# First attention's weights: turned by TensorE, or by VectorE and transfers

## The chip, the cores and the metric

One core of a Trainium2 chip runs the kernel once. The metric is the device time of that execution in microseconds. The kernel before took 1275.75 us as the median of three runs (1275.66 to 1276.08). Its engines are TensorE (matmuls and their weight loads, output in PSUM), VectorE, ScalarE and GpSimd, each with a queue of instructions of its own that it works through in order; SyncE (SP) and ScalarE also issue transfers to the DMA engines from their queues. Engines wait for each other at semaphores that are counted up.

## The reference

Two blocks of a model on 512 tokens of width 1024, all float32. What matters here is the first block's attention, 8 heads of 64:

```python
for i in range(t // Q_BLOCK):                     # 4 query blocks of 128
    ctx = (i + 1) * Q_BLOCK
    z = einsum("bhqd,bhkd->bhqk", q_blk, k[:, :, :ctx]) * scale
    mask = k_pos[None, :] < q_pos[:, None]
    log_1m_beta = where(mask, log_sigmoid(-z), 0.0)
    cs = cumsum(log_1m_beta, axis=3)
    log_a = log_sigmoid(z) + (cs[..., -1:] - cs)
    a = where(mask, exp(log_a), 0.0)
    outs.append(einsum("bhqk,bhkd->bhqd", a, v[:, :, :ctx]))
```

Beside it the same block computes, from the same normed input, a gated projection (branch A: gelu, layer norm, a mixing over 128 tokens), a causal convolution of 31 taps over 512 channels (branch B), three gates per channel, and later a feed-forward part. The second block is not touched.

## The kernel before

Every large product is a split one: a float32 operand is divided into a high part (ScalarE's copy with rounding, `hi`, L708) and a low part (VectorE's difference, `lo`, L1160), and three matmuls are added (`split_mm`, L1905). Weights come in transfers of 1 MB on SP's queue, two units to a transfer, into two halves of STAGE; a transfer waits until the low part before it in the same half is made (L530). High and low parts stand in rings of four units: `hi(n + 4)` waits for unit n to be done, and TensorE's unit n + 4 waits for both parts.

The order of the work is written out by hand on each engine, one step for each unit. In the stretch around the change the units are the twelve of P, G and U (U_B, i = 0 to 11, banks 0 and 1 in turn) and then branch A (`branch(0)`: two halves q of six units r, four gate units and two quads that use BH and BL). The steps of first attention are threaded into them. There are 12 steps s, three for each pair p of heads (s = 3p, 3p + 1, 3p + 2), of 384, 384 and 512 columns for each head of the pair (`STEP_W`, L124). One step goes through these hands:

- TensorE, behind unit s + 1: `pair_scores(s)` (L2042) into banks 2 and 3, once the sigmoids of step s - 1 have been read from them.
- VectorE: `pair_mask(s)` (L1372); ScalarE: `pair_sigmoids(s)` (L805), 1 - beta into GB and beta into BT, two buffers each; VectorE: `pair_scan(s)` (L1384), the running product from the right, into RS; GpSimd: BT times RS (L654), the attention weights with queries on the partitions.
- TensorE, behind unit s + 3: `pair_turn(s)` (L2059) turns them in 6 or 8 tiles of 128x128 into banks 4 and 5; ScalarE: `pair_turned(s)` (L815) copies them into AT, keys on the partitions.
- TensorE, behind units 6, 9, 12 and 15: `pair_values(p)` (L2071) multiplies with VATT; ScalarE: `pair_out(p)` (L832) copies into ATT, which is branch(1)'s operand.

The units are numbered on through: 12 to 17 are the first half of branch A, 18 is r = 0 of its second half. Between these VectorE drains each unit out of PSUM (times RBC), and works through the 124 taps of the convolution (`taps`, L1340): so many in each step, given by the literals at L1429 and L1472. ScalarE does the gate activations with a table load where the function changes (L852). `gates_first` (L2131) follows behind branch(1), with the layer norm over the convolution.

Of the kernel before, what the change touches and what calls it, by code (L numbers as in the profile page):

```python
# [27 lines left out]
ALU = mybir.AluOpType  # L28
# [124 lines left out]
def program(nc, x, ln1_g, w_in, b_gate, sg_ln_g, sg_ln_b, sg_w, sg_b, w_a_out, cv_w, cv_b, cv_ln_g,  # L153
# [11 lines left out]
    with ExitStack() as ctx:  # L165
# [41 lines left out]
        RS = at("RS", [P, 2, SEQ], F32, 108)  # L207
        AT = at("AT", [P, 2, 1920], F32, 207)
# [64 lines left out]
        def sem(name):  # L273
# [36 lines left out]
                                                  sem("sc_scan"))  # L310
        a_ready, at_t, at_ready, av_done, att_read = (sem("a_ready"), sem("at_t"), sem("at_ready"),
# [3 lines left out]
        c_sum, c_mean, c_cent, c_sq, c_ssum, c_var, c_ve, c_sd, c_norm, c_ready = (  # L315
            sem("c_sum"), sem("c_mean"), sem("c_cent"), sem("c_sq"), sem("c_ssum"), sem("c_var"),
            sem("c_ve"), sem("c_sd"), sem("c_norm"), sem("c_ready"))
# [113 lines left out]
        def _(sp):  # L431
# [83 lines left out]
            for p, src in enumerate(transfers()):  # L515
# [29 lines left out]
                if p == U_B // 2 + 2:  # L545
                    qk_load(1)
                if p == 2:
# [65 lines left out]
        def _(pool):  # L613
# [30 lines left out]
            pool.wait_ge(rb_done, 1)  # L644
            pool.memset(SS[:], 0.0).then_inc(ss_clear, 1)

# [3 lines left out]
            for s in range(12):  # L650
# [3 lines left out]
                pool.tensor_tensor(b, b, RS[:, :, 0:STEP_W[s % 3]], ALU.mult).then_inc(a_ready, 1)  # L654
            squares(1)
# [38 lines left out]
        def _(act):  # L694
# [120 lines left out]
            def pair_turned(s):  # L815
                ty = s % 3
                act.wait_ge(at_t, s + 1)
                if ty == 0 and s:
                    act.wait_ge(av_done, s // 3)
                if ty == 0:  # L820
                    act.activation(AT[:, :, 0:256], PS[:, 4:6, 0:256], ACT.Copy).then_inc(at_ready, 1)
                    act.activation(AT[:, :, 512:640], PS[:, 4:6, 256:384], ACT.Copy).then_inc(at_ready, 1)
                else:
                    nk, c0 = ty + 2, 128 * (ty + 1)
                    act.activation(AT[:].rearrange("p a (k c) -> p a k c", c=384)[:, :, 0:nk, c0:c0 + P]
                                   if ty == 1 else
                                   AT[:, :, 384:384 + 384 * nk].rearrange("p a (k c) -> p a k c", c=384)
                                   [:, :, :, 0:P],
                                   PS[:, 4:6, 0:nk * P].rearrange("p a (k c) -> p a k c", c=P),
                                   ACT.Copy).then_inc(at_ready, 1)  # L830
# [24 lines left out]
            for b in range(2):  # L855
# [6 lines left out]
                for q in range(2):  # L862
                    for r in range(6):
                        n = U_C + 12 * b + 6 * q + r
                        hi(n + 4)
                        if b == 0 and q == 0 and r < 4:
                            stick_act(12 + r)
                        if q == 0 and r == (1, 0)[b]:
                            if b:
                                act.wait_ge(unit_done, n)  # L870
                            else:
                                act.wait_ge(sc_scan, 12)
                            act.activation(BH[:], src[:], ACT.Copy).then_inc(bh_ready, 1)
# [6 lines left out]
            for p in range(10):  # L880
# [20 lines left out]
                if p == 4:  # L901
                    act.wait_ge(c_ve, 1)
# [247 lines left out]
        def _(dve):  # L1150
# [232 lines left out]

            def pair_scan(s):  # L1384
# [16 lines left out]
            for i in range(12):  # L1401
# [15 lines left out]
                if 2 <= i < 13:  # L1417
                    pair_mask(i - 1)
                lo(U_B + i + 4)
# [8 lines left out]
                if i >= 4:  # L1428
                    taps(3 if i < 6 else 4)  # L1429
# [10 lines left out]
            for b in range(2):  # L1440
                for q in range(2):
                    for r in range(6):
# [29 lines left out]
                        taps((4, 4, 4, 4, 6, 3)[r])  # L1472

            assert taps_done == KW * CVK
            for p in range(10):
                if p < 9:
                    dve.wait_ge(unit_done, U_C + 24 + p + 1)
                if p < 8:
                    if p < 4:
                        dve.wait_ge(drained, DR_C + 28 + p + 1)  # L1480
                    else:
                        dve.wait_ge(av_done, 4)
                        dve.wait_ge(at_ready, 16)
# [14 lines left out]
                if p == 3:  # L1498
# [5 lines left out]
                    dve.tensor_tensor(TG0[:], TG0[:], UU[:, 3, :], ALU.add).then_inc(c_ssum, 1)  # L1504
                if p == 4:
                    dve.wait_ge(c_var, 1)
                    dve.tensor_scalar(TG0[:], PS[:, 5, :], 1.0 / W, EPS, ALU.mult, ALU.add)\
                       .then_inc(c_ve, 1)
# [392 lines left out]
        def _(pe):  # L1901
# [157 lines left out]
            def pair_turn(s):  # L2059

                pe.wait_ge(a_ready, s + 1)
                if s:
                    pe.wait_ge(at_ready, s + (s + 2) // 3)
                else:
                    pe.wait_ge(sg_read, 4)
                for par in range(2):
                    for z in range(STEP_W[s % 3] // P):
                        last = tr(PS[:, 4 + par, z * P:(z + 1) * P], BT[s % 2][:, par, z * P:(z + 1) * P])
                last.then_inc(at_t, 1)

            def pair_values(p):  # L2071

                pe.wait_ge(at_ready, 4 * p + 4)
# [324 lines left out]
```

## Time and profile before

| | before |
|---|---|
| median of three runs | 1275.75 us |
| profiled execution, its own time | 1275.76 us |
| its span, first to last instruction | 1274.0 us |
| TensorE matmul busy | 1263.9 us, 99% |
| VectorE busy | 869.3 us, 68% |
| ScalarE busy | 586.3 us, 46% |
| GpSimd busy | 88.1 us, 7% |
| mean of the DMA engines (the queue of SP and ScalarE) | 40.7% |

Busy time is an average over stages with different limits. The span in 40 slices of 31.85 us shows them, in tenths of each slice (9 is 90% or more):

```
PE   8999999999999999999999999999999999999998
DVE  5489899899877776666666333675469998655544
ACT  7235466232263443333333223512368899444223
DMA  7556222422322333323322222249825555665421
```

PE is TensorE, DVE VectorE, ACT ScalarE. The stage of the change is in slices 4 to 8.

### The profile page before, as it was taken

To read this page: it belongs to the slowest core of one execution; us is meant where nothing else is said; L and a number is where in the kernel's file an instruction comes from. 1 tells how busy PE (TensorE), PEld (TensorE's weight loads), DVE (VectorE), ACT (ScalarE), POOL (GpSimd) and SP (SyncE) were. 2 spreads that over 40 slices of the span, in tenths; PEclk is the share of its full clock that TensorE was granted. 3 is DMA by queue.
4 is the path that set the end of the run, shared out by engine and by line. 5 is a ranking of instruction groups with operands and counts; after the bars stand their busy time and mean duration, and the time that the engine had idled before them with its cause. 6 is when DMAs were issued, how large, how long until landed. Compare 5 with 4: busy or idle time off the path is not lost.

```text
span 1274.0 us, 15378 instructions
## 1 busy us (share of the span) xinstructions
PE 1263.9 (99%) x5760; PEld 1016.6 (80%) x5760; DVE 869.3 (68%) x1164; ACT 586.3 (46%) x866; POOL 88.1 (7%) x68
## 2 busy tenths in 40 slices
PE   8999999999999999999999999999999999999998
PEld 7888777888888888888888888888877777777886
DVE  5489899899877776666666333675469998655544
ACT  7235466232263443333333223512368899444223
POOL 0000222000000200000000001300012220000000
PEclk9999999999999999999999999999999999999999
DMA  7556222422322333323322222249825555665421
GB/s 264 178 130 172 66 67 67 165 97 77 120 75 97 99 100 99 99 99 99 98 91 102 90 88 91 99 125 215 239 76 124 140 159 131 183 148 149 161 70 67
DMA packets 220922, 153.36 MB, mean 120 GB/s; under 512 B 119704, under 2 KB 196416, under 8 KB 220608
## 3 DMA queue, kind: packets, MB, share of 16 engines
q1 hardware_dynamic: 220272, 151.53, 40.7%
q10 hardware_dynamic: 592, 1.05, 0.2%
q8 instruction: 37, 0.61, 0.2%
q14 instruction: 21, 0.17, 0.0%
HBM read 134.21 MB, written 18.35 MB: 120 GB/s over the span
## 4 chain that ended last, share of the span: by engine, by line
PE 97%; DVE 1%; DMA 1%; ACT 0%; SPq 0%; issue 0%; ACTq 0%
PE PS L1903 97%; PE PS L1970 1%; DMA STAGE<-in_w_in 1%; DVE WL L1163 0%; DVE XL L1201 0%; DVE XG L1193 0%; ACT XH L744 0%; ACT WH L716 0%; DVE TB L1752 0%; DVE XT L1896 0%; ACT SQF L1133 0%; DVE XT L1891 0%; DVE BLR L1790 0%; SPq L521 0%; SPq L520 0%
## 5 line engine op out<-in xcount | busy, mean ns | idle before, releaser
L716 ACT ACTIVATE WH<-STAGE 128x1024 fp32r<-128x1024 f32 x214 | 225.9, 1058 | 540.2 <-PE PS L1903 528.6
L1903 PE MATMUL PS<-XH,WH 128*128 128x512 f32 x960 | 380.9, 397 | 0.0
L1163 DVE TENSOR_TENSOR WL<-STAGE,WH 128x1024 fp32r<-128x1024 f32 x214 | 275.4, 1289 | 147.8 <-ACT WH L716 147.4
L1903 PE MATMUL PS<-XH,WL 128*128 128x512 f32 x960 | 373.9, 389 | 0.0
L1903 PE MATMUL PS<-XL,WH 128*128 128x512 f32 x960 | 373.8, 389 | 0.0
L1903 PEld LDWEIGHTS PS<-XH,WH 128*128 128x128 f32 x960 | 180.2, 188 | 43.5 <-issue 5.5
L1903 PEld LDWEIGHTS PS<-XL,WH 128*128 128x128 f32 x960 | 180.3, 188 | 39.0 <-issue 2.6
L1903 PEld LDWEIGHTS PS<-XH,WL 128*128 128x128 f32 x960 | 180.2, 188 | 38.1
L1903 PE MATMUL PS<-WH,XH 128*128 128x512 f32 x224 | 88.1, 393 | 0.6 <-DVE WL L1163 0.6
L1903 PE MATMUL PS<-WH,XL 128*128 128x512 f32 x224 | 87.2, 389 | 0.0
L1903 PE MATMUL PS<-WL,XH 128*128 128x512 f32 x224 | 87.2, 389 | 0.0
L1354 DVE SCALAR_TENSOR_TENSOR CACC<-CPAD,VEC,CACC 128x512 f32<-128x512 f32 x120 | 84.3, 765 | 0.0
L1579 DVE TENSOR_TENSOR UPB<-PS,RBC 128x512 f32<-128x512 f32 x44 | 30.4, 690 | 70.7 <-PE PS L1903 70.6
L1903 PE MATMUL PS<-FH,WH 128*128 128x512 f32 x176 | 68.5, 389 | 0.0
L1903 PE MATMUL PS<-FL,WH 128*128 128x512 f32 x176 | 68.5, 389 | 0.0
L1903 PE MATMUL PS<-FH,WL 128*128 128x512 f32 x176 | 68.5, 389 | 0.0
L639 POOL TENSOR_TENSOR SS<-SS,SQ 128x512 f32<-128x512 f32 x16 | 22.7, 1420 | 572.2 <-ACT SQ L725 572.2
L1903 PEld LDWEIGHTS PS<-WH,XH 128*128 128x128 f32 x224 | 42.1, 188 | 9.8 <-ACT XCM L738 1.0
L1903 PEld LDWEIGHTS PS<-WL,XH 128*128 128x128 f32 x224 | 42.1, 188 | 8.8 <-issue 0.2
L1903 PEld LDWEIGHTS PS<-WH,XL 128*128 128x128 f32 x224 | 42.0, 188 | 8.8
L932 ACT ACTIVATE YB<-UPB,VEC 128x512 f32<-128x512 f32 x44 | 35.3, 803 | 12.1 <-DVE UPB L1579 12.1
L1903 PEld LDWEIGHTS PS<-FH,WL 128*128 128x128 f32 x176 | 33.0, 188 | 6.9
(289 smaller groups left out, 1782.3 us busy)
## 6 DMA issues: line engine op xcount, KB each, us to landing
STAGE<-in_w_in SPq DMA_DIRECT2D x51, 1024.0 KB, 5.2
STAGE<-in_w_up SPq DMA_DIRECT2D x22, 1024.0 KB, 5.1
STAGE<-in_w_down SPq DMA_DIRECT2D x11, 1024.0 KB, 5.0
probabilities<-TB SPq DMA_DIRECT2D x48, 128.0 KB, 5.8
PT<-probabilities SPq DMA_DIRECT2D x18, 256.0 KB, 5.6
STAGE<-in_w_out SPq DMA_DIRECT2D x4, 1024.0 KB, 5.3
STAGE<-in_w_rnn_out SPq DMA_DIRECT2D x4, 1024.0 KB, 5.3
STAGE<-in_w_attn_out SPq DMA_DIRECT2D x4, 1024.0 KB, 5.3
```

What stands on the lines that cost most here:

```text
L639: pool.tensor_tensor(SS[:], SS[:], SQ[:], ALU.add).then_inc(ss_added, 1)
L716: act.activation(ring(WH, n), staged(n), ACT.Copy).then_inc(hi_done, 1)
L932: act.activation(YB[:, r, :], UPB[:, r, 4:516], ACT.Identity, scale=VEC[:, bass.ds(V_FW[2] + c, 1)], bias=VEC[:, bass.ds(V_FB + c, 1)]).th ...
L1163: dve.tensor_tensor(ring(WL, n), staged(n), ring(WH, n).bitcast(F32), ALU.subtract)\
L1354: ins = dve.scalar_tensor_tensor(CACC[:, c, :], CPAD[:, c, 2 + j:2 + j + SEQ], col(V_CVW + KW * j + c), CACC[:, c, :], ALU.mult, ALU.add)
L1579: dve.tensor_tensor(UPB[:, r, 4:516], PS[:, r, :], RBC[:], ALU.mult)\
L1903: return pe.matmul(out_, lhsT, rhs, start=start, stop=stop, skip_group_check=True)
L1970: return pe.transpose(out_, in_, IDENT[:])
```

## The change

In a few words: "First attention's weights turned by VectorE and transfers, loaded through ScalarE's queue, three tiles in turn; tokens stay unscaled, fourteen taps moved". TensorE's turn and ScalarE's copies go. VectorE transposes BT in blocks of 32x32 into BTT (three tiles in turn and a fourth for step 11) in its step s + 3; SP stores each tile with 128-byte pieces to memory, four DMAs a step, behind the transfers p = 13 to 19; ScalarE waits for the three stores of a pair and loads them into AT with eight DMAs, in units 7, 10, 13 and 16. The values move to units 9, 12, 15 and 18, with bank 3 in place of 6 for pair 2. Two taps a unit stand where three or four did, five where four did. The clearing of SS is moved behind the last product on GpSimd, since BTT0 lies over it, and some semaphores of the convolution's norm are merged.

```diff
+        BTT = [at("BTT0", [P, 1024], F32, 91), at("BTT1", [P, 1024], F32, 175), at("BTT2", [P, 1024], F32, 184),
+               at("BTT3", [P, 1024], F32, 100)]
+        AROW = [nc.dram_tensor(f"attention_rows{i}", [1024, P], F32, kind="Internal").ap()
+                for i in range(12)]
+        def pair_tile(s):
+            return BTT[3 if s == 11 else s % 3][:, 0:2 * STEP_W[s % 3]]
...
+            def at_store(s):
+                sp.wait_ge(at_t, s + 1)
+                for a in range(4):
+                    sp.dma_start(AROW[s][0:2 * STEP_W[s % 3]].rearrange("(b i) (a j) -> a i b j", i=32, j=32)[a],
+                                 pair_tile(s)[32 * a:32 * a + 32].rearrange("p (b j) -> p b j", j=32))\
+                      .then_inc(at_out[s % 3], 16)
...
+                step = p - U_B // 2 - 5
+                if 0 <= step < 7:
+                    for s in ((0,), (1, 2), (3, 4), (5, 6), (7, 8), (9, 10), (11,))[step]:
+                        at_store(s)
...
+            def at_load(p):
+                for i in range(3):
+                    act.wait_ge(at_out[i], 64 * (p + 1))
+                if p:
+                    act.wait_ge(av_done, p)
+                for s in range(3 * p, 3 * p + 3):
+                    w = STEP_W[s % 3]
+                    for par in range(2):
+                        rows_ = AROW[s][par * w:(par + 1) * w].rearrange("(k p) c -> p k c", p=P)
+                        if s % 3 == 0:
+                            act.dma_start(AT[:, par, 0:256].rearrange("p (k c) -> p k c", c=P), rows_[:, 0:2])\
+                              .then_inc(at_ready, 16)
+                            act.dma_start(AT[:, par, 512:640], rows_[:, 2]).then_inc(at_ready, 16)
...
             def pair_out(p):
                 act.wait_ge(av_done, p + 1)
-                act.activation(ATT[:, p, :], PS[:, (6, 7, 6, 2)[p], :], ACT.Copy).then_inc(att_read, 1)
+                if p == 2:
+                    act.wait_ge(at_out[1], 64 * 4)
+                act.activation(ATT[:, p, :], PS[:, (6, 7, 3, 2)[p], :], ACT.Copy).then_inc(att_read, 1)
             def stick_act(i):
                 if 1 <= i < 13:
                     pair_sigmoids(i - 1)
-                if i >= 6 and i % 3 == 0:
-                    pair_out(i // 3 - 2)
-                if 3 <= i < 15:
-                    pair_turned(i - 3)
+                if i >= 9 and i % 3 == 0:
+                    pair_out((i - 9) // 3)
+                if i >= 7 and i % 3 == 1:
+                    at_load((i - 7) // 3)
...
+            def pair_turn(s):
+                w = STEP_W[s % 3]
+                dve.wait_ge(a_ready, s + 1)
+                if s >= 3:
+                    dve.wait_ge(at_out[s % 3], 64 * (s // 3))
+                dve.transpose(pair_tile(s).rearrange("p (a c) -> p a c", c=w), BT[s % 2][:, :, 0:w])\
+                   .then_inc(at_t, 1)
...
                 if 2 <= i < 13:
                     pair_mask(i - 1)
+                if i >= 3:
+                    pair_turn(i - 3)
                 lo(U_B + i + 4)
...
-                    taps(3 if i < 6 else 4)
+                    taps(2)
...
+                        if b == 0 and q == 0 and r < 3:
+                            pair_turn(9 + r)
                         lo(n + 4)
...
+                            if b == 0 and q == 0:
+                                for k in range(3):
+                                    dve.wait_ge(at_out[k], 64 * 4)
...
-                        taps((4, 4, 4, 4, 6, 3)[r])
+                        taps((5, 5, 5, 5, 5, 3)[r])
...
             def pair_values(p):
-                pe.wait_ge(at_ready, 4 * p + 4)
-                if p == 2:
-                    pe.wait_ge(att_read, 1)
-                if p == 3:
+                pe.wait_ge(at_ready, 128 * p + 128)
+                if p >= 2:
                     pe.wait_ge(sig_ready, 24)
...
-                if i >= 6 and i % 3 == 0:
-                    pair_values(i // 3 - 2)
-                if 3 <= i < 15:
-                    pair_turn(i - 3)
+                if i >= 9 and i % 3 == 0:
+                    pair_values((i - 9) // 3)
```

## Rows read from the trace of the kernel before

**Rows 1.** The page's part 4, by line: the chain that ended last.
```profile
PE PS L1903 97%; PE PS L1970 1%; DMA STAGE<-in_w_in 1%; DVE WL L1163 0%; DVE XL L1201 0%; DVE XG L1193 0%; ACT XH L744 0%; ACT WH L716 0%; DVE TB L1752 0%; DVE XT L1896 0%; ACT SQF L1133 0%; DVE XT L1891 0%; DVE BLR L1790 0%; SPq L521 0%; SPq L520 0%
```

**Rows 2.** Timeline of TensorE: start us, us, engine, line, operation, count.
```profile
111.43 0.93 PE L1903 MATMUL PS<-QKT 64*128 64x128 f32 x8
112.28 0.50 PE L1903 MATMUL PS<-XH,WH 128*128 128x512 f32 x1
...
136.29 0.93 PE L1903 MATMUL PS<-QKT 64*128 64x128 f32 x8
...
137.77 0.47 PE L1903 MATMUL PS<-XH,WH 128*128 128x512 f32 x1
...
143.43 0.92 PE L1903 MATMUL PS<-QKT 64*128 64x384 f32 x4
...
145.13 0.48 PE L1903 MATMUL PS<-XH,WH 128*128 128x512 f32 x1
...
200.13 2.37 PE L1903 MATMUL PS<-AT,VATT 128*64 128x512 f32 x16
...
208.64 0.82 PE L1970 MATMUL PS<-IDENT,BT 128*128 128x128 f32 x6
...
214.78 1.04 PE L1970 MATMUL PS<-IDENT,BT 128*128 128x128 f32 x8
...
221.23 2.37 PE L1903 MATMUL PS<-AT,VATT 128*64 128x512 f32 x16
```

**Rows 3.** Busy time in one stretch: PE, PEld, DVE, ACT, POOL, clock, DMA share, GB/s.
```profile
129.04:223.37 94.33, 94.33 (x484) 69.28 (x484) 86.24 (x111) 59.58 (x71) 22.51 (x11) 1.00 0.21 68
```

**Rows 4.** Timeline of VectorE.
```profile
71.75 2.48 DVE L1262 STREAM_TRANSPOSE QK<-QK 128x512 f32<-128x512 f32 x4
...
162.02 1.22 DVE L1163 TENSOR_TENSOR WL<-STAGE,WH 128x1024 fp32r<-128x1024 f32 x1
...
168.20 0.67 DVE L1410 TENSOR_TENSOR TG<-PS,RBC 128x512 f32<-128x512 f32 x1
...
169.12 2.23 DVE L1163 TENSOR_TENSOR WL<-STAGE,WH 128x1024 fp32r<-128x1024 f32 x1
...
171.88 2.73 DVE L1354 SCALAR_TENSOR_TENSOR CACC<-CPAD,VEC,CACC 128x512 f32<-128x512 f32 x4
...
176.24 0.66 DVE L1410 TENSOR_TENSOR TG<-PS,RBC 128x512 f32<-128x512 f32 x1
...
208.02 3.54 DVE L1354 SCALAR_TENSOR_TENSOR CACC<-CPAD,VEC,CACC 128x512 f32<-128x512 f32 x2
```

**Rows 5.** Timeline of GpSimd.
```profile
168.44 1.83 POOL L654 TENSOR_TENSOR BT<-BT,RS 128x768 f32<-128x768 f32 x1 [7.38 <-DVE RS L1395]
```

**Rows 6.** Timeline of ScalarE.
```profile
186.67 1.28 ACT L811 ACT_TABLE_LOAD   x1
187.97 0.81 ACT L811 ACTIVATE GB<-PS 128x768 f32<-128x768 f32 x1
...
191.50 0.63 ACT L852 ACTIVATE TG<-TG 128x512 f32<-128x512 f32 x1
```

**Rows 7.** Timeline of SP's queue: the time is that of the issues.
```profile
225.22 0.37 SPq L531 DMA_DIRECT2D STAGE<-in_w_a_out x1
...
986.44 0.39 SPq L531 DMA_DIRECT2D STAGE<-in_w_in  x1
...
987.97 5.93 SPq L477 DMA_DIRECT2D probabilities<-TB  x4
```

**Rows 8.** Busy time in one stretch, as rows 3.
```profile
994.00:996.00 2.00, 2.00 (x8) 1.08 (x6) 1.97 (x5) 1.99 (x7) 0.00 (x0) 1.00 0.75 123
```

**Rows 9.** ScalarE's own DMAs: issue ns (min/median/max), then KB and us to landing.
```profile
L1145 ACTq DMA_DIRECT2D out<-XT x4: 350/368/383, 1257.7 to 1270.8; - x4
...
out<-XT ACTq DMA_DIRECT2D x4, 256.0 KB, 2.6
```

**Rows 10.** Span and mean granted TensorE clock.
```profile
core 0: 1274.0 us, clock 0.999
```

More of the change, by code:

```diff
@@ L314, in program @@
         tg_act, tg_used = sem("tg_act"), sem("tg_used")
-        c_sum, c_mean, c_cent, c_sq, c_ssum, c_var, c_ve, c_sd, c_norm, c_ready = (
-            sem("c_sum"), sem("c_mean"), sem("c_cent"), sem("c_sq"), sem("c_ssum"), sem("c_var"),
-            sem("c_ve"), sem("c_sd"), sem("c_norm"), sem("c_ready"))
+        c_sum, c_mean, c_cent, c_sq, c_sd, c_norm, c_ready = (
+            sem("c_sum"), sem("c_mean"), sem("c_cent"), sem("c_sq"),
+            sem("c_sd"), sem("c_norm"), sem("c_ready"))
         bh_ready, bl_ready = sem("bh_ready"), sem("bl_ready")
@@ L654, in _ @@
                 pool.tensor_tensor(b, b, RS[:, :, 0:STEP_W[s % 3]], ALU.mult).then_inc(a_ready, 1)
+            pool.wait_ge(at_out[0], 64 * 4)
+            pool.memset(SS[:], 0.0).then_inc(ss_clear, 1)
             squares(1)
@@ L813, in pair_sigmoids @@
                 act.activation(BT[s % 2][:, :, 0:w], PS[:, 2:4, 0:w], ACT.Sigmoid).then_inc(sig_ready, 1)
[L815 to L830, printed above, removed]
+            def at_load(p):
[11 more added lines that the diff above has]
+                            act.dma_start(AT[:, par, 512:640], rows_[:, 2]).then_inc(at_ready, 16)
+                        elif s % 3 == 1:
+                            act.dma_start(AT[:, par, 0:1152].rearrange("p (k c) -> p k c", c=384)[:, :, 256:384],
+                                         rows_).then_inc(at_ready, 16)
+                        else:
+                            act.dma_start(AT[:, par, 384:1920].rearrange("p (k c) -> p k c", c=384)[:, :, 0:P],
+                                         rows_).then_inc(at_ready, 16)
@@ L865, in _ @@
                         hi(n + 4)
-                        if b == 0 and q == 0 and r < 4:
-                            stick_act(12 + r)
+                        if b == 0 and (q == 0 or r == 0):
+                            stick_act(12 + 6 * q + r)
                         if q == 0 and r == (1, 0)[b]:
@@ L872, in _ @@
                                 act.wait_ge(sc_scan, 12)
+                                act.wait_ge(at_out[2], 64 * 3)
                             act.activation(BH[:], src[:], ACT.Copy).then_inc(bh_ready, 1)
@@ L901, in _ @@
                 if p == 4:
-                    act.wait_ge(c_ve, 1)
+                    act.wait_ge(c_sum, 3)
                     act.activation(TG0[:], TG0[:], ACT.Sqrt).then_inc(c_sd, 1)
@@ L2057, in pair_scores @@
                 last.then_inc(sc_done, 1)
[L2059 to L2069, printed above, removed]
             def pair_values(p):
-                pe.wait_ge(at_ready, 4 * p + 4)
-                if p == 2:
-                    pe.wait_ge(att_read, 1)
-                if p == 3:
+                pe.wait_ge(at_ready, 128 * p + 128)
+                if p >= 2:
                     pe.wait_ge(sig_ready, 24)
@@ L2080, in pair_values @@
                         h = 2 * p + par
-                        last = mm(PS[par * DH:(par + 1) * DH, (6, 7, 6, 2)[p], kb * P:SEQ],
+                        last = mm(PS[par * DH:(par + 1) * DH, (6, 7, 3, 2)[p], kb * P:SEQ],
                                   VATT[:, kb, h * DH:(h + 1) * DH], AT[:, par, 512 * kb:384 * kb + SEQ],
@@ L2118, in branch @@
                             pe.wait_ge(drained, DR_C + 16 * b + 8 * q - 8 + r + 1)
+                            if b == 0 and r == 2:
+                                pe.wait_ge(att_read, 4)
                         cm_unit(n0 + 6 * q + r, r % 2 if b == 0 and q == 0 else r, XH, XL)
-                        if b == 0 and q == 0:
-                            stick_pe(12 + r)
+                        if b == 0 and (q == 0 or r == 0):
+                            stick_pe(12 + 6 * q + r)
                     if b == 0 and q == 0:
-                        pe.wait_ge(att_read, 3)
+                        pe.wait_ge(att_read, 2)
                     if q == 0:
@@ L2140, in gates_first @@
                     if p == 4:
-                        pe.wait_ge(c_ssum, 1)
-                        mm(PS[:, 5, :], ONES[:], TG0[:], True, True).then_inc(c_var, 1)
+                        pe.wait_ge(c_sum, 2)
+                        mm(PS[:, 5, :], ONES[:], TG0[:], True, True).then_inc(c_mean, 1)
                 pe.wait_ge(c_cent, KW)
-                pe.wait_ge(c_ve, 1)
+                pe.wait_ge(c_sum, 3)
                 pe.wait_ge(bh_ready, 3)
```

10 lines of the change are left out of this document (4 added, 6 removed).

## The prediction

> **What bounds the kernel now.** I read the chain that ended last first. It is TensorE for 97% of the span in its split matmuls and another 1% in its transposes [rows 1]. So a microsecond of TensorE work that goes is a microsecond of time, unless another engine or a transfer becomes late. The second view is TensorE's own order of work around first attention [rows 2]. The stage runs in channel-major units of 24 matmuls (5.45 us). Behind unit i stand the scores of step i-1, every third time the values of a head pair, and the transposes of step i-3. I count the units on: 0 to 11 are the P, G and U columns, 12 to 17 the first half of branch 0, 18 the first of its second half. The third view is VectorE, which does one step of work per unit. From its drain of unit 3 (129.04) to its drain of unit 15 (223.37) it is busy 86.2 us of 94.3 [rows 3], and at the end of the stretch it is behind: unit 15 is done at 221.23 [rows 2] and drained 2.1 us later. TensorE never waits for it, but little is free there. ScalarE and the queues come last in the reading.
>
> **Off TensorE.** With 6 tiles the turn lies between scores and unit: 136.29 to 137.77 against 111.43 to 112.28 where none stands, 1.48 less 0.85, so 0.63. With 8 tiles it is 143.43 to 145.13 less 0.85, so 0.85. Alone between units, 208.64 to 214.78 less a unit is 0.69, and 214.78 to 221.23 less a unit is 1.00 [rows 2]. Seven of the first, three of the second and the last two make 8.65 us. All twelve lie on the path. The values move three units later (2.3 us each, the same sixteen matmuls), which costs nothing by itself. Of the path 8.65 us go, if nothing is late.
>
> **On VectorE.** 12 transposes come in. Four of 128x512 take 2.48 us one behind another, 0.62 each [rows 4]; by width that is 0.93 and 1.24 us for 768 and 1024 columns, of which some 0.07 lies over the neighbour: 8 x 0.87 and 4 x 1.16, 11.6 us (bounds 8 and 16). A tap is 0.66 (2.73 for four) [rows 4]. Two a unit in place of three or four is 14 fewer up to unit 11, 9.2 us; five in place of four gives one back in each of the units 12 to 14.
>
> There is a third term. The weights' low part (two SBUF operands) takes 2.23 us when GpSimd's product runs beside it, against 1.22 alone; the drain just before it, with one operand in PSUM, keeps 0.67 beside the same product [rows 4, 5]. In the new order a transpose stands between mask and low part, so GpSimd is through (1.83 us) before the low part begins. The nearest row for a one-operand instruction is that drain, so I let the transpose keep its time: some 1 us less in each of units 8, 9, 11 and 0.5 in 10 and 12. If it is stretched instead, as the low part is, those 4 us come back on VectorE and reach TensorE at pair 3: 1277.9 in place of the sum below. The Trainium skill, "SBUF — State Buffer", section "Who interferes with whom", says that a VectorE instruction with two SBUF inputs contends with a GpSimd instruction that reads SBUF, and one with at most one SBUF input doesn't, outside the two-port modes. By that the transpose is free of it, which is the case that I take from the drain's row; the trace agrees for low part and drain and shows no transpose there.
>
> **Step by step.** A unit's period is 6.5 us with scores (143.43 less 136.29 less 0.63), 6.7 behind the 512-wide scores, 9.0 where values stand as well, and 5.45 alone. Unit 5 ends at 142.1 (143.43 less two turns), and then units 6 to 10 at 148.6, 155.3, 161.8, 168.3, 177.3 and 11 at 183.8. VectorE's step behind unit 8 took 8.04 us (168.20 to 176.24) [rows 4]; less 1.3 for two taps and 1.0 for the low part, with 1.16 for the transpose, it is 6.9, and its neighbours come out at 6.7 to 7.5 in the same way; it starts them at 142.5, 149.3, 156.1, 163.3, 170.2, 177.4, 184.5. It keeps up.
>
> **ScalarE's queue.** It now holds the loads behind the sigmoids in units 7, 10, 13 and 16: eight DMAs each time. An issue on this queue was 0.37 us for 256 KB [rows 9], on SP's 0.37 to 0.39 for weights and 1.5 for the stores of second attention behind a full ring [rows 7]; I take 0.45, so 3.6 us (bounds 3.0 and 7). Removed are the copies out of PSUM of the same units. In unit 7 nothing is late. In unit 10 the sigmoids end at 177.3 + 5.1, the loads at 186.0, and the table load and Gelu of that unit (1.28 and 0.55) [rows 6] at 187.9. Only then come the next high part (188.9), table load and two sigmoids of 0.75 [rows 6]: 191.7. TensorE wants them for its scores when unit 12 ends, at 190.3: **1.4 us of stall** (bounds 0 and 4). VectorE waits for that high part too and starts step 12 at about 194.4.
>
> Step 12 on VectorE has drain, mask, transpose, low part, the 512-wide scan and five taps of which two run beside GpSimd's product (3.54 us for two in the same place before, 1.4 alone) [rows 4], and a wait for the sigmoids: 11.7 us, so step 13 starts at 206.1. Unit 13 ends at 190.3 + 1.4 + 9.0 = 200.7. Step 13 takes 8.1 us (BL's low part in it, five taps, a transpose), step 14 6.2. Unit 15 needs the drain of unit 13 (206.7) and could start at 206.2: 0.4 us more (bounds 0 and 2). So step 15 starts at 220.4, with unit 15 done at 212.0. That step's low part, done at 222.2, releases the weights' transfer and behind it on SP's queue the store of the last step, as it released the transfer at 225.22 before [rows 7].
>
> **The last round trip.** The values of pair 3 stand behind unit 18, which ends at 212.0 + 2.35 (values 2) + 3 x 5.45 = 230.7. They need the last store, then the loads. Nearest is second attention's: weights issued 986.44, two loads of 256 KB, four stores with 4096 packets of 128 bytes, the DMA engines through at about 995.5 (busy 0.75 of 994 to 996) [rows 7, 8]. Less 1.4 for those loads that is 7.7 us from the low part. The eight loads: the last is issued 3.2 us later and lands 2.6 after that, as ScalarE's stores did [rows 9]; 5.8. Landed at 222.2 + 7.7 + 5.8 = 235.7: **5.0 us of stall** (bounds 0, if VectorE is 5 us earlier, and 10, if the loads meet a full ring as the four stores did, 5.93 us for four issues in place of 1.8 [rows 7]). ScalarE stands still meanwhile, from about 221 to 234, its high part for unit 21 among what is behind, but that is not wanted before 248. The earlier loads of pair 2 (their stores land near 200, their wait begins near 202) are in time, and BH with its low part comes 3 us before its quads. The stall lets VectorE catch up by as much, and from the quads on it has fewer instructions a unit than 5.45 us hold, so the taps that were moved there (2 us more in each half branch) stay hidden; without that cover they would cost those 2 us.
>
> Removed semaphores, other banks for pair 2 (3 in place of 6), SS cleared later and the merged c_* waits change no order on a busy path; zero, bounds -0.3 and +0.3. The diff holds no edit of how tokens are scaled, so nothing is counted for it.
>
> Sum: 8.65 gained, 1.4 + 0.4 + 5.0 lost, 1.85 left. The profiled execution took 1275.76 us around its span of 1274.0, the runs' median is 1275.75; so 1275.76 - 1.85 = **1273.9 us**.
>
> **The rivals.** First, VectorE and ScalarE have room after all: drains that start late but never stop TensorE, issues of 0.37, a shorter last trip. For it: TensorE waited nowhere before, and VectorE had 8.1 us of idle time in the stretch [rows 3]. Against: TensorE comes 8.65 us sooner, which takes up all of that idle time. With 2 us of stalls in all it gives 1269.1.
>
> Second, on the other side, the load on ScalarE's queue: it waits in order for stores that wait behind weights and behind VectorE, and holds back high parts and TensorE alike. The point from which it decides is a trip of 15.4 us from the low part of step 15 to the last landing, where I have 13.5: the stall at pair 3 is then 6.9 and the gain is gone. At 20 us, which a full ring (7 us of issues) and stores 3 us slower would give, it is 11.5 and the time 1280.4. For it: four such stores held SP's queue for 5.93 us [rows 7], and what waits for them now waits on the engine that feeds TensorE. Against: the loads have a queue of their own, with nothing ahead of them.
>
> Third, TensorE's clock. It was granted 0.999 of full over the span [rows 10], which is some 3 us at the lower of its two levels, and in the stage it was 1.00 with TensorE never idle. A stop of 5 us behind unit 18 has no like in this trace after the start. If the lower level (1.2 GHz) followed for half a unit or for a whole one, the matmuls, 0.227 us apart now, would be at least twice 0.21 apart: 2.4 to 4.8 us, time 1276.3 to 1278.7. The Trainium skill, "TensorE: Matmul & The Clock Gate", section "HAM oscillation — how this bites in real kernels", holds that an idle gap in mid-kernel can send the clock back to the lower level; no row of before can show it.
>
> **How the numbers follow.** The forecast has 0.45, around 1273.9, itself from 1271.5 to 1276.3; the first rival 0.20; ScalarE's queue 0.20; the clock 0.15. What a measurement can tell from no change is 0.2%, 2.55 us, so faster means under 1273.2. The forecast gives 0.19 to faster, 0.26 to the same; the first rival 0.20 to faster; the second 0.01 to the same and 0.19 to slower; the third 0.11 to the same and 0.04 to slower. Together 0.39, 0.38, 0.23. The range leaves out the tails of both ends: 1269.3 to 1279.
>
> **What would show it.** No TensorE transposes after 30 us, the chain in pieces of 6.5 us. A gap of TensorE of 5 us ahead of the values of pair 3, released by a DMA into AT, and one of 1.4 ahead of the scores behind unit 12, released by ScalarE. VectorE's transposes at 0.9 and 1.2 beside GpSimd, and low parts of 1.2 behind them. ScalarE's eight issues at 0.45. A granted clock under 1.00 behind the gap speaks for the third rival. The forecast is wrong if the gaps sum to under 4 or over 9 us, or if a gap stands at another place, the quads of branch 0 above all.

## The result, and the profile after

The changed kernel takes **1279.34 us** (median of 9 runs, 1278.46 to 1280.84), the kernel before beside it 1275.61 (9 runs, 1275.32 to 1276.08): ratio 1.0029, 95% interval [1.0020, 1.0038]. It is 3.7 us slower. The forecast was 1.85 us faster; the measured time lies just outside its range. The profiled execution took 1280.36 us around a span of 1278.6.

The first views of the kernel after, answering to [rows 10] and [rows 1] (span and clock; the chain by line):
```profile
core 0: 1278.6 us, clock 0.995
```
```profile
PE PS L1945 93%; DMA STAGE<-in_w_in 1%; DVE CACC L1381 0%; DVE WL L1190 0%; SPq L508 0%; DMA attention_rows<-BTT 0%; ACTq L850 0%; DMA AT<-attention_rows 0%; DVE XL L1228 0%; DVE XG L1220 0%; ACT WH L736 0%; ACTq L848 0%; ACTq L853 0%; ACT XH L764 0%; ACTq L846 0%
```
The transposes (1% of the chain before) are gone, but TensorE's share fell from 97% to 93%: the chain now leaves it for VectorE, SP's queue, two transfers and ScalarE's queue. Where it leaves it, the waits of TensorE say (us in total, times, longest), and its timeline, which answers to [rows 2]:
```profile
PE PS L1945 <- DMA AT<-attention_rows: 6.5, 1, 6.5
PE PS L1945 <- ACT BT L833: 2.2, 1, 2.2
```
```profile
192.92 1.67 PE L1945 MATMUL PS<-QKT 64*128 64x512 f32 x4 [2.25 <-ACT BT L833]
194.52 3.48 PE L1945 MATMUL PS<-AT,VATT 128*64 128x512 f32 x16
197.93 0.50 PE L1945 MATMUL PS<-XH,WH 128*128 128x512 f32 x1
...
214.48 2.37 PE L1945 MATMUL PS<-AT,VATT 128*64 128x512 f32 x16
...
239.86 4.54 PE L1945 MATMUL PS<-AT,VATT 128*64 128x512 f32 x16 [6.47 <-DMA AT<-attention_rows]
244.33 0.60 PE L1945 MATMUL PS<-XH,WH 128*128 128x512 f32 x1
```
Two stops stand there, at the two places that the prediction named. But look at the durations too: the same sixteen matmuls of a pair's values take 2.37, 3.48 and 4.54 us, and the scores 1.67 where they take 1.13 in the stage otherwise. The clock granted in those microseconds (the column behind the five engines) explains it:
```profile
192.00:193.00 1.00, 0.08 (x2) 0.08 (x2) 1.00 (x2) 0.98 (x3) 0.00 (x0) 1.00 0.61 70
193.00:194.00 1.00, 1.00 (x4) 0.22 (x4) 1.00 (x2) 1.00 (x1) 0.00 (x0) 0.69 0.86 276
194.00:196.00 2.00, 2.00 (x6) 0.52 (x6) 2.00 (x4) 1.23 (x3) 0.92 (x1) 0.50 1.08 364
196.00:197.00 1.00, 1.00 (x6) 0.37 (x4) 1.00 (x3) 0.62 (x1) 1.00 (x1) 0.61 1.37 215
197.00:198.00 1.00, 1.00 (x13) 0.49 (x7) 1.00 (x2) 0.55 (x1) 0.21 (x1) 1.00 1.50 187
...
237.00:238.00 1.00, 0.00 (x0) 0.00 (x0) 0.03 (x1) 1.00 (x2) 0.00 (x0) 0.87 0.87 254
238.00:244.00 6.00, 4.14 (x16) 1.72 (x16) 6.00 (x9) 0.82 (x1) 0.00 (x0) 0.50 0.86 278
244.00:245.00 1.00, 1.00 (x6) 0.59 (x3) 1.00 (x2) 0.55 (x2) 0.00 (x0) 0.71 1.18 492
```
0.50 is the lower level, 1.2 GHz. Behind the first stop the clock fell during the scores and came back before the values were through (0.61 at 196, 1.00 at 197); at the second it fell while TensorE still stood, and came back behind the values.

**The balance.** Set the starts of the split matmuls of both kernels side by side, the first with the first, and read where the difference changes. It falls by 0.6 or 0.84 at each turn that is gone, in all by 8.4 us. At the start of unit 12 it is -8.50: nine turns (6.2), and one pair's values (2.3), which now come later. At unit 13 it is -5.14: a stop of 2.25 and 1.6 at the lower clock, less a turn of 0.6. At unit 15 it is -6.75. At unit 19 it is +4.56: the values that moved here (2.3), the stop of 6.5, 2.2 at the lower clock, and 0.3 left over. From there to the end nothing changes any more. The turns gave 8.4; the stops took 8.7 and the clock 3.8, and some 0.5 at the stops is not put down to any row: +4.6, which is the difference of the two spans.

### The profile page after: what moved, and what is told of

Same layout as the page of the kernel before. It is cut to its first block, busy times and chain, and to the rows that moved or that the text cites. A ratio compares the mean times of both kernels' runs of the same rounds, so it can differ in the third digit from the quotient of the medians.

```text
span 1278.6 us, 15300 instructions
## 1 busy us (share of the span) xinstructions
PE 1260.3 (99%) x5680; PEld 1010.1 (79%) x5680; DVE 875.4 (68%) x1176; ACT 576.3 (45%) x850; POOL 88.5 (7%) x68
## 4 chain that ended last, share of the span: by engine, by line
PE 93%; DVE 2%; DMA 1%; ACTq 1%; ACT 1%; SPq 1%; issue 0%
PE PS L1945 93%; DMA STAGE<-in_w_in 1%; DVE CACC L1381 0%; DVE WL L1190 0%; SPq L508 0%; DMA attention_rows<-BTT 0%; ACTq L850 0%; DMA AT<-attention_rows 0%; DVE XL L1228 0%; DVE XG L1220 0%; ACT WH L736 0%; ACTq L848 0%; ACTq L853 0%; ACT XH L764 0%; ACTq L846 0%
## 5 line engine op out<-in xcount | busy, mean ns | idle before, releaser
L1190 DVE TENSOR_TENSOR WL<-STAGE,WH 128x1024 fp32r<-128x1024 f32 x214 | 271.0, 1269 | 148.7 <-ACT WH L736 148.4
L1945 PEld LDWEIGHTS PS<-FH,WH 128*128 128x128 f32 x176 | 33.0, 188 | 6.9
```

The source lines that it names most:

```text
L1190: dve.tensor_tensor(ring(WL, n), staged(n), ring(WH, n).bitcast(F32), ALU.subtract)\
L1945: return pe.matmul(out_, lhsT, rhs, start=start, stop=stop, skip_group_check=True)
```

## The experiments

Each time stands beside runs of the kernel before on the same chip, 1275.8 to 1276.0 in all of them; ratios are to these. The kernel after was measured twice, with 1279.34 and, further below, 1280.89 us, so a difference of about 1 us between kernels that keep a stop is not read as a gain or a loss. Traces begin up to 1.2 us apart ahead of the stage: where two are set side by side, both are counted from their first scores (111.42 in the kernel after).

### Matmuls that keep TensorE busy in both stops

```diff
+            def fill(n, bank):
+                for _ in range(n):
+                    mm(PS[:, bank, :], XH[:, 0, 0:P], XH[:, 0, :], True, True)
...
             def stick_pe(i):
+                if i == 12:
+                    fill(9, 4)
+                if i == 18:
+                    pe.wait_ge(att_read, 3)
+                    fill(26, 3)
```


> The changed kernel with needless matmuls (0.227 us each) in TensorE's two gaps: 9 ahead of the scores behind unit 12, 26 ahead of the values of pair 3. Nothing else is changed, and the two waits stay as they are. First theory (two stops, and the clock falls in each): the gaps stay as long in sum, filled now, the granted clock stays 1.00 in both places, and the 1.6 and 2.2 us that scores and values took longer at the lower level come back, so 1279.3 - 3.8 = 1275.5. Rival (the longer values and scores are slowed by something else, transfers or PSUM, and the clock's level only stands beside it): no change, 1279.3. If the filling reaches past a gap, up to 0.5 us is lost.

Measured 1279.83 us (6 runs), ratio 1.0033 [1.0020, 1.0045]: no gain. TensorE in that trace:
```profile
193.27 1.13 PE L1945 MATMUL PS<-QKT 64*128 64x512 f32 x4 [0.32 <-ACT BT L833]
194.33 2.37 PE L1945 MATMUL PS<-AT,VATT 128*64 128x512 f32 x16
...
208.58 0.50 PE L1945 MATMUL PS<-XH,WH 128*128 128x512 f32 x1 [0.78 <-DVE GS L1487]
...
233.01 6.05 PE L1945 MATMUL PS<-XH 128*128 128x512 f32 x26
...
240.91 2.38 PE L1945 MATMUL PS<-AT,VATT 128*64 128x512 f32 x16 [1.85 <-DMA AT<-attention_rows]
```
The clock stayed at 1.00 and scores and values have their full speed, so the stops do cause the lower clock. But the 3.8 us did not come back. Half of the first 1.6 went at unit 15, where TensorE now came early enough to wait 0.78 us for VectorE's drain of unit 13 (GS). The rest only makes TensorE wait longer at pair 3, where the end of the stop is set by a transfer: AT landed at 240.9 in place of 239.8, or 0.8 later from the first scores on. Of the second 2.2, this landing took 0.8 and 0.9 more went at 1085 us of the span, in the second attention, where TensorE waited 1.6 for VectorE's BLR in place of 0.6.

### The stores ahead of the wait for the low part

```diff
+                step = p - U_B // 2 - 5
+                if 0 <= step < 7:
+                    for s in ((0,), (1, 2), (3, 4), (5, 6), (7, 8), (9, 10), (11,))[step]:
+                        at_store(s)
                 if p >= 2:
                     sp.wait_ge(lo_done, 2 * p - 2)
                 sp.dma_start(STAGE[:, p % 2, :].rearrange("p (k c) -> p k c", k=kd, c=ncol), src)\
...
-                step = p - U_B // 2 - 5
-                if 0 <= step < 7:
-                    for s in ((0,), (1, 2), (3, 4), (5, 6), (7, 8), (9, 10), (11,))[step]:
-                        at_store(s)
```


> The changed kernel with each store of attention rows issued ahead of the weights' transfer of its place, so it waits for its own transpose only and not for VectorE's low part and 1 MB of weights. First theory (the stop at pair 3 is the round trip low part, weights, store, load): store 11 leaves at 218 in place of 224.7, the loads end at about 231, before unit 18 ends at 233.3, so the gap of 6.5 us and the 2.2 us of lower clock go; the gap behind unit 12 stays (2.3 + 1.6): 1279.3 - 8.9 = 1270.4. Rival (the volume of small packets on the DMA engines, 5.2 MB in 128 bytes, is what is late): the same bytes in another order, 1279.3 within 1 us. Second rival (VectorE's lag itself): the gap shrinks by under 3 us.

Measured 1270.21 us (4 runs), ratio 0.9954 [0.9938, 0.9971]: 5.7 us faster than before, 9.1 than the kernel after, where 1270.4 was expected. At pair 3 the difference to the kernel before now changes by 2.37 us, the values alone: no stop. With the same bytes in another order this also rules out the rival of DMA volume. The way there was not as expected. TensorE waits for AT behind unit 9 now, 1.1 us, and as it comes that much later and ScalarE's sigmoids 1.2 earlier, the stop behind unit 12 is gone as well; 0.7 appears at unit 15, on VectorE's drain. So the mechanism at pair 3 is confirmed, and that the number fits to 0.2 us is partly luck.

### The loads on SP's queue

ScalarE's eight issues (`at_load`) go to SP, behind the stores that they wait for; nothing else is changed.
```diff
-                if i >= 7 and i % 3 == 1:
-                    at_load((i - 7) // 3)
...
-                        at_store(s)
+                    for kind, k in ((("s", 0),), (("s", 1), ("s", 2), ("l", 0)), (("s", 3), ("s", 4)),
+                                    (("s", 5), ("l", 1), ("s", 6)), (("s", 7), ("s", 8), ("l", 2)),
+                                    (("s", 9), ("s", 10)), (("s", 11), ("l", 3)))[step]:
+                        (at_store if kind == "s" else at_load)(k)
```


> The changed kernel with the loads of attention rows issued by SP's queue in place of ScalarE's, the stores where they were. First theory (the stop behind unit 12 is ScalarE's 4 us of issues ahead of a high part and two sigmoids): that gap of 2.3 us goes with its 1.6 us of lower clock; VectorE comes some 3 us earlier too, so the gap at pair 3 stays 6.5 to 7.5 us, with its lower clock: 1279.3 - 3.3 = 1276.0. Rival (the sigmoids are late because VectorE's mask and transpose are late): the gap behind unit 12 stays over 1.5 us, and 1279.3 stays.

Measured 1278.79 us (10 runs), ratio 1.0021 [1.0011, 1.0031]; 1276.0 was expected. TensorE's waits and the values of pair 3:
```profile
PE PS L1945 <- DMA AT<-attention_rows: 6.9, 1, 6.9
PE PS L1945 <- ACT BT L856: 1.4, 3, 0.8
```
```profile
238.42 4.21 PE L1945 MATMUL PS<-AT,VATT 128*64 128x512 f32 x16 [6.86 <-DMA AT<-attention_rows]
```
The stop behind unit 12 shrinks to 0.8 and its clock stays up, so ScalarE's issues were the greater part of its cause. It is worth little by itself. TensorE waits 0.3 us for the sigmoids behind units 10 and 11 too, and 0.8 at unit 15 for VectorE's drain. Unit 18 ends 1.3 us earlier, counted from the first scores, but the trip takes 16.0 us here (low part done at 222.4, last load landed at 238.4), and so the stop at pair 3 grows from 6.5 to 6.9 and brings the lower clock again. The expectation had that stop and its clock, but neither the longer trip nor the small waits; the median is only 0.55 us below the kernel after, which the two measurements of that kernel do not tell from nothing.

### Both

```diff
+                    for kind, k in ((("s", 0),), (("s", 1), ("s", 2)), (("s", 3), ("s", 4)),
+                                    (("s", 5), ("l", 1), ("s", 6)), (("s", 7), ("s", 8)),
+                                    (("s", 9), ("s", 10)), (("s", 11), ("l", 3)))[step]:
+                        (at_store if kind == "s" else at_load)(k)
                 if p >= 2:
                     sp.wait_ge(lo_done, 2 * p - 2)
```
The loads of pairs 0 and 2 stand behind the transfers of steps 1 and 4.

> Both edits: stores ahead of the weights' transfers and loads on SP's queue. First theory: no stop of TensorE is left in the stage, the clock stays at 1.00, and what was taken off TensorE (8.4 us) is the whole difference: 1275.6 - 8.4 = 1267.2 (to 1268.5 if a wait of under 1 us shows up). Rival (DMA volume, or VectorE as the bound): a gap of 3 us or more remains and the time is over 1271.

Measured **1267.92 us** (4 runs), ratio 0.9936 [0.9920, 0.9953]: 8.0 us faster than before, and the fastest version of all. TensorE waits nowhere in the stage:
```profile
190.71 1.13 PE L1949 MATMUL PS<-QKT 64*128 64x512 f32 x4
191.76 2.37 PE L1949 MATMUL PS<-AT,VATT 128*64 128x512 f32 x16
...
229.90 2.38 PE L1949 MATMUL PS<-AT,VATT 128*64 128x512 f32 x16
```
With no stop left, the balance against the kernel before is the 8.4 us of the turns less some 0.6 in small steps. So the turns are worth their time and VectorE can carry its transposes; what ate the gain was the order of stores and loads on two queues.

### The last store alone

```diff
+                step = p - U_B // 2 - 5
+                if 0 <= step < 7:
+                    for s in ((0,), (1, 2), (3, 4), (5, 6), (7, 8), (9, 10), (11,))[step]:
+                        if s in (11,):
+                            at_store(s)
                 if p >= 2:
                     sp.wait_ge(lo_done, 2 * p - 2)
...
-                        at_store(s)
+                        if s not in (11,):
+                            at_store(s)
```


> The kernel after with one line of order changed: SyncE issues the last store of attention_rows (of step 11 alone) ahead of its wait for the low part of step 14 and the transfer of the weights, the ten stores before it stay where they were. Theory (pair 3's values wait for a round trip that runs low part, weights, store, load): the stop of 6.5 us ahead of them goes, and with it the 2.2 us that they took longer at the lower clock, while the stop of 2.3 us ahead of the scores behind unit 12 stays, being ScalarE's eight load issues. 1279.3 - 9.0 = about 1270.5 us. Rival (all the stores together were what held, by filling SyncE's queue): the stop at pair 3 shrinks by 1 or 2 us only, about 1278. Rival (the stop behind unit 12 hangs on the stores too): it goes as well, about 1268 to 1269.

Measured 1270.72 us (5 runs), ratio 0.9962 [0.9948, 0.9976]; 1270.5 was expected. One store's place is worth 8.6 us. Its trace holds a surprise:
```profile
192.96 1.13 PE L1951 MATMUL PS<-QKT 64*128 64x512 f32 x4 [2.14 <-ACT BT L839]
194.02 2.37 PE L1951 MATMUL PS<-AT,VATT 128*64 128x512 f32 x16
```
The stop behind unit 12 is there, 2.1 us, and the clock did not fall. So this kernel and the kernel after were each run again.

> The kernel with the last store alone ahead of the transfer of the weights, a second time, for its granted clock behind unit 12. If the clock there stands by the stop's place in time and not by its length, the scores and values may take 5 us in this execution where they took 3.4 in the first. Otherwise 3.4 us again. The time is near 1270.7 us, or 1.6 more with the lower clock.

> The kernel after, unchanged, a second time. Theory that the stop of 2.3 us behind unit 12 always brings the lower clock: the scores and values behind it take 5 us again and the granted clock is near 0.50 from 194 to 196 us. Rival, since the kernel with the last store first had a stop of 2.1 us there at a granted clock of 1.00: whether such a short stop brings it differs from execution to execution, and here it may be 3.4 us. In either case the stop of 6.5 us at pair 3 brings it again, and the median is 1279 to 1280 us.

The last store first, a second time, took 1271.66 us (one run):
```profile
192.28 1.13 PE L1951 MATMUL PS<-QKT 64*128 64x512 f32 x4 [2.28 <-ACT BT L839]
193.34 4.07 PE L1951 MATMUL PS<-AT,VATT 128*64 128x512 f32 x16
```
```profile
194.00:196.00 2.00, 2.00 (x8) 0.61 (x6) 2.00 (x5) 1.22 (x2) 1.56 (x1) 0.50 1.18 305
```
Here it fell, for the same instructions in the same order. The kernel after, a second time, had 1280.89 us (5 runs), ratio 1.0037 [1.0022, 1.0051], a stop of 2.15 with the clock at 0.50 behind it, and 8.2 at pair 3. So a stop of some 2.2 us brings the lower level in four of the five traces that have one there, and not in the fifth. Its length does not set the fifth apart: one of 2.06 us behind unit 9, in a run below, brought it too. What does is left open.

### Matmuls in one stop only

Nine ahead of the scores behind unit 12, on top of the last store first:
```diff
             def stick_pe(i):
+                if i == 12:
+                    fill(9, 4)
```


> The kernel of the run before (last store first), with nine more matmuls of 128x512 f32r ahead of the scores behind unit 12, into a bank that nobody reads then; they compute nothing that is used. Theory that the lower clock in the scores and values behind unit 12 is time lost: with no round trip behind it that eats the gain, the scores and values take 3.4 us instead of 5.0 and the time falls by about 1.3 to 1.6 us against the run before. Rival (the time from there on is set by VectorE's or the transfers' row, not by TensorE): within 0.5 us of the run before.

And the 26 ahead of pair 3's values, on top of the kernel after:
```diff
             def stick_pe(i):
+                if i == 18:
+                    pe.wait_ge(att_read, 3)
+                    fill(26, 3)
```


> The kernel after with 26 more matmuls of 128x512 f32r ahead of the values of pair 3 alone, into a bank that nobody reads then; the stop behind unit 12 is left as it was. They compute nothing that is used and end before the load of AT lands, so they move no transfer. Theory that the values of pair 3 pay for the lower clock in time: they take 2.4 us instead of 4.5, and the time falls by 2 us against the kernel after, to about 1277.3 us. Rival (what is won here is lost again at the round trip of the second attention's probabilities, near 1085 us of the span, where both kernels with filler so far came 0.9 to 1.2 us later): 1278 to 1279.5 us.

The first took 1271.34 us (5 runs), ratio 0.9966 [0.9952, 0.9981], no better than without them, though its profiled clock is 1.00 behind unit 12; its trace also has 0.9 us more at 1085 us. The two traces of the last store first show the price of that fall better, as their program is the same. The one in which it fell is 1.7 us later at unit 13 and only 0.7 later behind unit 15, mostly since there the other waits 0.78 for VectorE's drain; at pair 3 it waits 0.64 for AT and is 1.4 later from there on. The spans differ by 0.6 (1269.9 against 1269.3), as the traces begin 0.7 apart. One execution each is little to go by. The second took 1279.77 us (10 runs, one of them a lone 2579.5 that stays unexplained), ratio 1.0028 [1.0018, 1.0038]: no clear gain, 1.1 us below the kernel after on the same chip (1280.89), in spreads that overlap. The fill was too short there:
```profile
232.51 6.05 PE L1945 MATMUL PS<-XH 128*128 128x512 f32 x26
241.25 4.07 PE L1945 MATMUL PS<-AT,VATT 128*64 128x512 f32 x16 [2.69 <-DMA AT<-attention_rows]
```
The 2.69 us that were left of the stop brought the lower clock back, so the trace did not test what it was made for, while the 1.85 us left in the run with both fills did not bring it. Its other executions say more: the five with a mean clock of 0.999 took 1277.8 to 1279.6 us, the four with 0.997 or 0.998 took 1280.0 to 1282.0. A longer stop makes both the time longer and a fall likelier, so this is no price of the clock alone.

### The fourteen taps

In the kernel before, moved as in the change:
```diff
-                    taps(3 if i < 6 else 4)
+                    taps(2)
...
-                        taps((4, 4, 4, 4, 6, 3)[r])
+                        taps((5, 5, 5, 5, 5, 3)[r])
```


> The kernel before with only the fourteen taps moved: two each of units 4 to 12, five each of the first five steps of the second branch. Attention's weights are turned by TensorE as before. Theory: TensorE doesn't wait for VectorE there, the taps run beside other work in either place, so no change, 1275.5 to 1276 us. Rival (the moved taps themselves make step 12 to 15 of VectorE late, and this is what the changed kernel pays): 1 to 4 us slower.

And in the kernel after, put back:
```diff
+                if s == 11:
+                    dve.wait_ge(at_t, 11)
...
-                    taps(2)
+                    taps(3 if i < 6 else 4)
...
-                        taps((5, 5, 5, 5, 5, 3)[r])
+                        taps((4, 4, 4, 4, 6, 3)[r])
```


> The kernel after with the fourteen taps where they were before (three or four a unit in units 4 to 12, four a step behind them), so the turns, transfers and loads stay and the move of the taps is undone. Theory: VectorE's steps 4 to 12 grow by 1.1 to 2.2 us each, the turns come later, ScalarE's loads behind unit 12 too, and TensorE waits there and at unit 13 longer than now: slower than the kernel after by 3 to 12 us, 1282 to 1291 us. Rival (VectorE's steps have room, and the round trip at pair 3 sets the time alone; the steps behind unit 12 are shorter with four taps): pair 3 is earlier, 1277 to 1279 us.

The added wait, of VectorE for its own turns before the last, changes no order. The first took 1275.89 us (10 runs), ratio 1.0001 [0.9992, 1.0011]: by itself the move does nothing. The second took 1285.08 (4 runs), ratio 1.0071 [1.0054, 1.0088], 5.7 us over the kernel after. TensorE's waits:
```profile
PE PS L1947 <- ACT BT L833: 6.0, 3, 3.3
PE PS L1947 <- DMA AT<-attention_rows: 5.9, 1, 5.9
```
Three stops behind ScalarE's sigmoids in place of one. So with these queues the transposes would not fit on VectorE without the move of the taps; both numbers are as they were expected.

## Why the prediction was wrong

**Off TensorE: right.** 8.65 us were forecast, 8.4 went. Nothing of the twelve turns was hidden.

**VectorE and the third term: right.** Transposes cost what their width says, and keep it beside GpSimd's product; the low part behind them meets only the product's end. VectorE and GpSimd in unit 8, against [rows 4, 5]:
```profile
170.89 0.97 DVE L1417 STREAM_TRANSPOSE BTT<-BT 128x768 f32<-128x768 f32 x1
171.78 1.33 DVE L1190 TENSOR_TENSOR WL<-STAGE,WH 128x1024 fp32r<-128x1024 f32 x1
```
```profile
170.20 1.83 POOL L672 TENSOR_TENSOR BT<-BT,RS 128x768 f32<-128x768 f32 x1 [4.95 <-DVE RS L1431]
```
0.97 was put at 0.93, and it is 0.96 at 208.11, where no product runs. The low part is 1.33 where it was 2.23, and 1.18 where nothing runs beside it. The rule of the Trainium skill's "SBUF — State Buffer", section "Who interferes with whom", holds here for the transpose, an operation that the trace before could not show.

**ScalarE's queue: 2.25 us in place of 1.4.** ScalarE in the kernel after, from the first load to the sigmoids for the scores behind unit 12:
```profile
183.12 0.37 ACTq L846 DMA_DIRECT2D AT<-attention_rows  x1
...
186.07 1.07 ACTq L853 DMA_DIRECT2D AT<-attention_rows  x2
187.17 1.28 ACT L878 ACT_TABLE_LOAD   x1 [4.16 <-issue]
...
192.06 0.80 ACT L833 ACTIVATE BT<-PS 128x768 f32<-128x768 f32 x1
```
The issues took 4.0 us (forecast 3.6, at 0.45 each; 0.50 measured) and began 0.7 later than forecast. The step is right in kind, and the run with the loads on SP confirms it. The 0.4 at unit 15 did not occur here, where TensorE came later by the stop and the lower clock; it did, with 0.71 to 0.78 us, in the five traces in which the clock stayed up and TensorE had waited at unit 9, 10 or 12 (both fills, all stores first, loads on SP, the last store first, and the same with one fill). So that term's mechanism was right, and it is what took half of the first fall of the clock back.

**The last round trip: the step that failed.** Its last load was to land at 235.7 and landed at 239.8, and the stop before it was 6.5 us in place of 5.0. The chain of waits in the kernel after, where it leaves TensorE (start us, us, what):
```profile
223.12 1.14 DVE WL L1190
...
224.28 0.39 SPq L548
...
224.72 0.51 SPq L508
...
225.27 0.56 SPq L508
...
225.87 3.48 SPq L508
...
229.39 3.16 DMA attention_rows<-BTT
...
232.70 0.37 ACTq L846
...
236.18 3.64 DMA AT<-attention_rows
...
239.86 10.31 PE PS L1945 x40
```
The low part ends at 224.26 (forecast 222.2), the last load lands at 239.8 (forecast 235.7): a trip of 15.6 us where 13.5 were put, and 16.1 in the second profile of the same kernel (16.0 to 16.9 in the other four that have it). To the last store's landing it is 8.3 (7.7), then 3.5 to the start of the last issue (3.2) and 3.6 from there to its landing (2.6): 7.3 with the step between, in place of 5.8. What the prediction calls a full ring no row shows; the rows show only that some issues take longer than others.

The trip began 2.1 us late, because VectorE was late. Its step 12 began 1.05 after the forecast's 194.4, behind the high part that ScalarE's issues had held back, and took 0.4 more; in step 13 it waited 0.57 for BH, which stood on ScalarE's queue behind the eight loads of pair 2 (1.72 in the second profile). The prediction had called those loads in time. With the first fall of the clock gone (the run with both fills) the low part ended only 0.6 earlier, counted from the first scores, so TensorE's own lateness is the smaller part of it. TensorE ended unit 18 at 233.4 in place of 230.7, so of the 4.1 us by which the load was late only some 1.5 show as a longer stop.

15.6 is past the point (15.4) that the second rival named for the gain to be gone, and the second rival is half of what happened: the queue that did harm was SP's, where the last store, ready at 218.1, stood behind the weights' wait until 224.7. The prediction saw that place and took it as given. It could have asked what those 6 us in front of the store cost.

**The clock: a rival at 0.15, and part of the outcome.** The third rival had 2.4 to 4.8 us for the stop at pair 3; 2.2 came, and 1.6 more behind the stop of 2.25, for which the prediction allowed nothing. In the sum of the forecast the clock stood at nothing. The rule named there, of the Trainium skill's "TensorE: Matmul & The Clock Gate", section "HAM oscillation — how this bites in real kernels", is borne out by both stops here; the stop of 2.14 that left the clock up shows that a gap of this length does not do it every time. As terms these are 3.8 of the 6.5 us between forecast and profiled execution; but the run that kept the clock up in both places won nothing, since behind the first stop it is TensorE's time against a drain and a transfer that aren't there yet. What the clock behind the second stop costs by itself stays open, as do the 0.7 to 0.9 us at 1085 us that all three kernels with extra matmuls show.

Put together term by term, the errors are 0.2 (turns), 0.85 (ScalarE), -0.4 (unit 15), 1.5 (last stop), 3.8 (clock) and 0.4 left over at the stops: 6.4 in all, against 1280.36 less 1273.9. Along the path that set the time it is shorter: the last load landed 4.1 us later than forecast and the values behind it took 2.2 longer, 6.3; what TensorE lost before mostly just shortened its stop. So the wrong sign does not hang on the clock. The late landing alone turns a gain of 1.85 into a loss of 2.3, and the kernel at full clock (both fills) was still 3.9 us slower than before. What it hangs on is the store's place: with the last store moved, nothing else, the kernel is 5.1 us faster than before.

## What to carry to other kernels

When work is taken off the bounding engine and given to a round trip over queues, follow each item in the queue back to the moment when its data was ready; here one store that stood 6.6 us behind an unrelated wait decided between 1279.3 and 1270.7 us, and the order of both queues between a loss of 3.7 and a gain of 8.0. A wait that holds back an engine's queue belongs behind everything in it that is ready. If the sum contains a stop of TensorE of 2 us or more, as here, its clock belongs into the sum and not only among the rivals; and what is won or lost ahead of a stop that a transfer ends is not won or lost in time.

## What was not expected of the hardware

- The granted clock fell to 0.50 behind stops as short as 2.06 (behind unit 9 in the run with the taps put back), 2.15, 2.16, 2.25, 2.28 and 2.69 us. It stayed at 1.00 behind stops of 1.12 and 1.85, and once behind one of 2.14, in the same place of a program in which it fell at 2.28.
- Four stores of 1024 rows in pieces of 128 bytes took 5.2 us to issue, 3.5 of them for the third alone, and the last of them landed 7.8 us after the first issue began (8.8 and 9.0 in two other traces); eight loads of 512-byte pieces took 4.0 us to issue and the last of them 3.6 to 4.2 to land. In unit 13 the same eight took 4.8 to issue (5.9 and 5.7 in two other traces), and where the weights' transfer was issued beside the last pair's loads they needed 5.6 and 5.8 to land.
- Where ScalarE's wait for the stores was over early, its eight issues began before the two activations ahead of them in its program and ran beside them; the next activation came only behind the last issue (186.47). ScalarE in the kernel with all stores first:
```profile
182.12 0.40 ACTq L846 DMA_DIRECT2D AT<-attention_rows  x1
...
183.19 0.81 ACT L831 ACTIVATE GB<-PS 128x768 f32<-128x768 f32 x1
...
183.90 0.80 ACT L833 ACTIVATE BT<-PS 128x768 f32<-128x768 f32 x1
```
